# A two-block transformer kernel: when the last layer's context scan keys are made, and how branch products are laid between scan steps

## What is computed

```
q_c, k_c, v_c = ...                      # context
o_cf, s_f = _gla_scan(qc, kc, vc, lfc, s0)
o_cb, s_b = _gla_scan(_flip(qc), _flip(kc), _flip(vc), _flip(lbc), s0)
o_lf, _ = _gla_scan(ql, kl, vl, lfl, s_f)
o_lb, _ = _gla_scan(_flip(ql), _flip(kl), _flip(vl), _flip(lbl), s_b)
...
br_a = ((a_b * _short_conv(a_c * a_x, conv_w_l)) * silu(a_z)) @ w_br_conv_l
```

## Time and profile before

| | before |
|---|---|
| median of 3 runs | 2311.36 us |
| the profiled execution | 2309.95 us |
| its span in the trace | 2307.9 us |
| TensorE busy | 2138.2 us, 93% of the span |
| TensorE weight loads | 1829.8 us, 79% |
| VectorE busy | 1321.8 us, 57% |
| ScalarE busy | 963.7 us, 42% |
| GpSimd busy | 555.7 us, 24% |
| mean granted clock of TensorE | 0.96 of full speed |
| DMA | 285.00 MB, mean 123 GB/s |

### The profile page before, as it was taken

The page is one execution under the profiler, slowest core; times in us unless marked ns, Lnnn a source line. Parts: engine busy times, 40 slices in busy tenths (PEclk is TensorE's granted clock), DMA queues, the critical chain, the costliest instruction groups (busy, mean ns, idle before and its releaser), DMA issues.

```text
span 2307.9 us, 31382 instructions
## 1 busy us (share of the span) xinstructions
PE 2138.2 (93%) x12074; PEld 1829.8 (79%) x12074; DVE 1321.8 (57%) x2200; ACT 963.7 (42%) x1602; POOL 555.7 (24%) x323
## 2 busy tenths in 40 slices
PE   7888998988999899999999999999989788989998
PEld 6668897766999688877887788888768688878997
DVE  5735666674777415638434456867361667565464
ACT  4434554443555424353323453232342553435443
POOL 1413333242333311011211002322231111320432
PEclk9979999988999999999999999999989899999999
DMA  9334665321455422212122115534323323341543
GB/s 250 126 136 167 232 217 201 128 91 65 160 180 190 133 92 73 82 46 73 65 95 87 47 37 175 182 102 138 120 78 126 101 83 110 110 147 46 174 146 129
DMA packets 79066, 285.00 MB, mean 123 GB/s; under 512 B 8822, under 2 KB 9730, under 8 KB 78920
## 3 DMA queue, kind: packets, MB, share of 16 engines
q1 hardware_dynamic: 70560, 256.15, 32.8%
q10 hardware_dynamic: 6072, 18.73, 2.3%
q0 software_dynamic: 2288, 8.13, 1.3%
HBM read 277.14 MB, written 5.83 MB: 123 GB/s over the span
## 4 chain that ended last, share of the span: by engine, by line
PE 40%; DVE 9%; ACT 4%; issue 2%; POOL 0%; POOLq 0%; DVEq 0%; ACTq 0%
PE pb L830 8%; PE pb L832 8%; PE pb L831 8%; PE pb L842 3%; PE pb L844 3%; PE pb L843 3%; PE pb L848 2%; PE pb L1156 2%; PE pb L1137 1%; ACT SPH L1277 1%; DVE GW L2105 1%; DVE SPL L1815 1%; PE pb L1053 1%; PE pb L1097 1%; DVE ATT L2133 1%
## 5 line engine op out<-in xcount | busy, mean ns | idle before, releaser
L1815 DVE TENSOR_TENSOR SPL<-RAW,SPH 128x1024 fp32r<-128x1024 f32 (+1 forms) x291 | 416.2, 1437 | 479.5 <-ACT SPH L1277 443.2
L2392 POOL TENSOR_TENSOR SPL<-RAW,SPH 128x1024 fp32r<-128x1024 f32 x171 | 418.6, 2450 | 1112.4 <-ACT SPH L1277 998.8
L830 PE MATMUL pb<-HTH,SPH 128*128 128x256 f32 (+1 forms) x1984 | 647.0, 326 | 8.1 <-DVE SPL L1815 3.9
L831 PE MATMUL pb<-HTL,SPH 128*128 128x256 f32 (+1 forms) x1984 | 636.9, 321 | 0.0
L832 PE MATMUL pb<-HTH,SPL 128*128 128x256 f32 (+1 forms) x1984 | 636.7, 321 | 0.0
L1277 ACT ACTIVATE SPH<-RAW 128x1024 fp32r<-128x1024 f32 x462 | 476.6, 1048 | 287.7 <-PE pb L844 130.2
L830 PEld LDWEIGHTS pb<-HTH,SPH 128*128 128x128 f32 x1984 | 381.7, 192 | 42.5 <-issue 14.1
L831 PEld LDWEIGHTS pb<-HTL,SPH 128*128 128x128 f32 x1984 | 382.1, 193 | 26.9
L832 PEld LDWEIGHTS pb<-HTH,SPL 128*128 128x128 f32 x1984 | 381.5, 192 | 27.1
L842 PE MATMUL pb<-SPH,HTH 128*128 128x512 f32 x544 | 222.0, 408 | 18.5 <-DVE SPL L1815 8.8
L844 PE MATMUL pb<-SPL,HTH 128*128 128x512 f32 x544 | 217.0, 399 | 0.0
(11 more groups left out here) (271 smaller groups left out, 2957.9 us busy)
## 6 DMA issues: line engine op xcount, KB each, us to landing
RAW<-in_w_up SPq DMA_DIRECT2D x88, 512.0 KB, 4.3
RAW<-in_wa SPq DMA_DIRECT2D x64, 512.0 KB, 3.2
RAW<-in_w_in SPq DMA_DIRECT2D x48, 512.0 KB, 5.3
RAW<-in_wmg SPq DMA_DIRECT2D x48, 512.0 KB, 3.2
RAW<-in_wbr SPq DMA_DIRECT2D x48, 512.0 KB, 3.2
RAW<-in_w_down SPq DMA_DIRECT2D x44, 512.0 KB, 3.5
RAW<-in_w_ada SPq DMA_DIRECT2D x24, 512.0 KB, 4.8
ARAW<-in_w_ada ACTq DMA_DIRECT2D x24, 512.0 KB, 4.0
```

Of the source, the lines that this page charges most:

```text
L830: T.matmul(o, wh[:, kt, :], xh[:, kt, n0:n1], start=kt == 0, stop=False)
L831: T.matmul(o, wh[:, kt, :], xl[:, kt, n0:n1], start=False, stop=False)
L1815: W.tensor_tensor(lo, raw, hi.bitcast(F32), SUB).then_inc(*dve.tick(s["lo_dve"], ("u", u)))
L2392: G.tensor_tensor(lo, raw, hi.bitcast(F32), SUB).then_inc(*pool.tick(s["lo_pool"], ("u", u)))
```

## The change

Four things, all for the last layer.

1. The generator of the scan is made before the value projections, and the table `KEYS` says how many of its steps follow each of the 8 value weight tiles: 3, 3, 1, 2, 2, 2, 2, 1, that is 16 steps: the context's `gdec`, `gln`, `ginit` and all of its `gwiden`. `gke` and `gst` stay in the weave. For layer 0 all eight numbers are 0.
2. The value projections take their banks from `LO4` in place of `ALL8` in the last layer, since `gdec` uses `HI4`.
3. The weave's ratio `RA[1]` goes from 1.8 to 1.25.
4. `IC[1]` goes from 5.5 to 5 and `PC[1]` from 13 to 15.

```diff
-RA = [2.0, 1.8]
-IC, PC = (4, 5.5), (8, 13)
+RA = [2.0, 1.25]
+IC, PC = (4, 5), (8, 15)
+KEYS = ((0,) * 8, (3, 3, 1, 2, 2, 2, 2, 1))
...
+        scan, steps = self.gla(l, HI4), iter(KEYS[l])
         for g in range(2):
-            drain(self.group_n(("gv", l, g), f"wgv{l}", g, (0, 1, 2, 3), ALL8, H))
+            for _ in self.group_n(("gv", l, g), f"wgv{l}", g, (0, 1, 2, 3), LO4 if last else ALL8, H):
+                for _ in range(next(steps)):
+                    next(scan)
             for t in range(4):
                 self.add("gv", l, g, t)
                 self.give(("gv", l, g, t))
         self.add("mark", f"br{l}")
-        weave(self.branch_a(l, LO4), self.gla(l, HI4), RA[l])
+        weave(self.branch_a(l, LO4), scan, RA[l])
```

## The result

The change made the kernel faster, by half of what was predicted. The changed kernel took 2296.49 us in the median (2292.97 to 2298.49), the kernel before 2310.99 beside it on the same chip: ratio 0.9938, 95% interval 0.9925 to 0.995. That is 14.3 us off the 2311.36 shown above, with an interval from 11.6 to 17.3. The prediction said 28.4 us off, 2283.0, and a range of 2278 to 2294.

A forecast was written before the change was run, and what follows sets the result against it. TensorE, busy 93% of the span, was taken to bound the kernel through its waits and low clock. 17.1 + 6.9 + 2.2 + 4.6 − 2.4 = 28.4 us off 2311.36 gave 2283.0 us, range 2278 to 2294.

The forecast's parts named there:

- The chain moved: Context's key chain beside the value projections, ending at about 1795 us: 14.7 us wait and 2.4 us clock go, 17.1 gained.
- The bank wait: At the fifth value tile, TensorE waits for a bank still to be copied by ScalarE: a new 2.4 us loss.
- No clock cost in the value projections: Beside the value projections TensorE is full at full clock, so no low-clock time was charged there.
- PC and the ratio: Latent `gln` to `ginit`, 12 branch steps in place of 8: L2090's 4.7 us wait and 2.2 us clock go, 6.9 gained.
- The split: Branch products' waits for a weight's low half, made on ScalarE behind latent `gln`: 3.9 us become 1.7, 2.2 gained.
- IC 5, four branch steps per level: Seven latent levels: VectorE 8.3 us per level against TensorE 7.9, 3 us of waits kept, 4.6 us gained.
- New idle stretches shorter than 3.4 us, so I charge no clock.: TensorE's new waits (2.4, 1.7, under 1 us a level) are below the shortest seen before a low clock: no charge.
- The rest of the program at nothing: Outside the value projections and scan stage, the sum had no term for any gain or loss.
- Rival 1: In the latent levels every GpSimd split holds VectorE for 2.38 us: 9.1 us per level, 2288 us, chance 0.2.
- Rival 2: Beside the values ScalarE is later: bank wait 3.9 us with low clock, 3.7 us less gained, 2287 us, chance 0.15.
- rivals 3 and 4: Respectively: stretched latent levels on VectorE, 2315 us, chance 0.03; key chain ending after TensorE already waits, 2292 us, chance 0.04.

The follow-up runs named there:

- the decays apart: Changed kernel with one decay step between two value tiles (table 1,1,1,1,3,3,3,3): 2299.77 us, ratio 0.9953.
- both edits of the levels: Changed kernel with ScalarE's key copy behind each latent level's first weight half and all the levels' splits on VectorE: 2282.87 us, ratio 0.9879.

## Why the prediction was wrong, step by step

- *The chain moved.* Right. The 14.7 us wait did not come back on another reader. Key products ran from 1782.85 to 1802.8 us, later than the 1795 laid out (2.5 us of it because the first value product itself started later in this execution) and still ahead of their use. The kernel with the chain's move alone gained 16.3 us in the stretch, against 14.7.
- *The bank wait.* Right: 2.00 us on L846 for L1479 at 1784.19 us, 2.4 predicted; the first branch product came 2.2 us earlier when the banks were changed.
- *No clock cost in the value projections.* Wrong. It took "TensorE is full" for "the clock stays": behind 12 thin products (33x256) in a row came a low stretch without any idle time, 1.8 us.
- *PC and the ratio, 6.9 us.* 5.1 came. The wait for L2090 (4.7 us) is 1.8 us now, put down to "issue". The rows name it: the two products of L2094 end at 1858.93 us, `gprod` starts at 1859.03, and the split ahead of them took 2.54 us, stretched beside GpSimd. That GpSimd split lies ahead of the levels and was not moved in any run, so that GpSimd is the cause of the 1.8 us is argued and not shown.
- *The split, 2.2 us.* Right in kind: 1.24 us left where 1.7 was kept.
- *IC 5, four branch steps per level, 4.6 us.* **This step failed.** The sum compared 8.3 us on VectorE with 7.9 on TensorE and took 3 us of waits and no clock; measured were 8.9 us per level, 6.0 us of waits for the queries' weights and 4.7 us of clock. That is 10.7 us against 7.6 before, a loss of 3.1 where a gain of 4.6 was booked. Its parts were right: own work, stretches (5.9 us in seven levels, 0.8 each, as taken), TensorE's pace (7.5 to 7.7 us per level, even a little under the 7.9). What it left out is that VectorE was idle for up to 1.7 us in a level, 4.5 us in seven, for a weight half that stood on ScalarE's queue behind a copy of VectorE's own result. With that copy moved and the stretches removed, 1.2 us of these waits are left and no clock.
- *"New idle stretches shorter than 3.4 us, so I charge no clock."* Wrong. Behind the shorter waits of before no row showed a low clock, and a handful of cases was taken for a bound. In the changed kernel 1.82 us of wait at 1892.22 were followed by a low stretch, in others 2.0 (at 1889.07 in the kernel with the chain's move alone) and 2.2 us; 2.0 us at 1784 were not.
- *The rest of the program at nothing.* 1.7 us were lost there by an added low stretch; the sum had no term for it.
- *Rival 1* (VectorE bound, by GpSimd's splits) was the nearest: its 9.1 us per level against 8.9. Half of its mechanism is shown: GpSimd's splits do hold VectorE. By the Trainium skill, page "SBUF — State Buffer", section "Who interferes with whom", the second of the two waits for all of the first; the three rows of GpSimd above agree. The key product at 1916.41 us ends 1.1 us after the split's end, as if it began there, and the two weight splits are longer by 1.1 and 1.3 us, about what was left of GpSimd's instruction when they came (1.2 and 1.5). But the rival gave 2288, since it too charged one clock drop of 1.4 us and no coupling. *Rival 2* (ScalarE late beside the values) is refuted, *rivals 3 and 4* did not occur.

With VectorE's two delays removed the kernel takes 2282.87 us, close to what the prediction said of the change itself, 2283.0. In part that is luck. Its stretch is 193.3 us against 192.3 by the prediction: the 1.8 us at the first weighted `gprod` and the 1.8 us of clock in the value projections, both taken as nothing, stand against 1.8 us less in the levels, 0.5 less at the split and 0.4 less at the bank wait.

## What to carry to other kernels

Before you take an engine's period to be its own work, follow in program order, for each of its inputs, what stands ahead of the producer on the producer's queue, and whether that waits for this very engine; a copy that waits for the result belongs behind the work that does not. Price every new wait of TensorE that is as long as the 1.8 us found here with the clock too, as a cost that may or may not come, and take rows that lack a case as no evidence on it. When a local edit is measured to 1 us or less, read the edited stretch in the profile and the rest of the span apart, since low stretches on untouched instructions move the total by as much as the edit; and let a median that meets its expectation count only if the edited stretch does too.

## What the runs showed of the hardware that was not expected

- TensorE's clock fell to 0.50 for 3.4 us behind 12 products of 33x256 in a row, with TensorE busy for all of the 2.7 us before, in all nine profiles that have them together beside the values; with 4 or 8 together it did not (three profiles).
- The same wait at the same instructions was followed by a low stretch in one kernel and not in another. The "issue" wait of 1.8 us at the first weighted `gprod` was followed by one in the five profiles where TensorE reached it without the bank wait (the four with the other banks and the one with the decays apart), and not in the other six that have it. The wait of 2.9 us behind the first `kv` product was met by one in eleven profiles, and not in the two of the kernel before and that of both edits of the levels. So here the length of a wait alone does not decide. Waits of 1.8, 2.0 and 2.2 us stand on either side; of 1.4 us and less none was followed by a low stretch in the scan stage.
- Behind the first `kv` product the same work took 335.3 to 339.5 us over fourteen profiles. Its first three long waits (2.9, 4.7 and 5.8 us) are the same in all, and the low stretches at them last nothing, 3.4 or 6.8 us. In the two kernels that were profiled twice the two times agree to 0.1 us, so it seems to go with the kernel and not with chance; what in a kernel decides it stays open. It is as large as most of the edits tried here.
- A VectorE instruction with two SBUF inputs that meets GpSimd's weight split ends as if it had been held until that split ends: 1.23 us became 3.33 where it came 0.12 us behind it. All four such meetings in the seven levels of the changed kernel look so. Without GpSimd's splits the same instruction took 1.23, and no instruction of VectorE in the levels was longer than its like.
